# Two network blocks in one kernel: unscaled activations in `w_up` and `w1_1`, and 32 units of the modulation added up by VectorE

## The reference, cut to what matters

```python
def rmsnorm(x, g):                       # r = rsqrt(mean(x*x) + EPS), one number a token
    return x * r * g
def conv_ffn(xn, w_up, conv_w, conv_b, w_down):       # xn = rmsnorm(h, norm_ffn_g)
    h = xn @ w_up                                     # 256 x 5632
    h = causal_conv3(h, conv_w) + conv_b              # per channel, over the tokens
    a, b = jnp.split(h, 2, axis=-1)
    return (jax.nn.silu(a) * b) @ w_down
# second block, two layers i = 0, 1
sx1, cx1, gx1, sx2, cx2, gx2 = split(silu(c) @ ada_w[i] + ada_b[i], 6)       # for x
sc1, cc1, gc1, sc2, cc2, gc2 = split(silu(c_ctx) @ ada_w[i] + ada_b[i], 6)   # for the context
x = x + gx2 * _mlp(_rms(x, norm_mlp_g[i]) * (1 + cx2) + sx2, mlp_w1[i], mlp_w2[i])
def _mlp(h, w1, w2):
    return jnp.square(jax.nn.relu(h @ w1)) @ w2
```

## Time and profile before

| | |
|---|---|
| median of 3 runs | 1424.33 us (1420.19 to 1426.97) |
| the profiled execution's own time | 1423.98 us |
| its span, first to last instruction | 1422.2 us |
| PE busy | 1366.4 us, 96% |
| DVE, ACT, POOL busy | 714.1, 604.7, 448.6 us |
| mean granted clock of TensorE | 0.989 of 2.4 GHz |
| `w_up` on PE | about 243 to 396 us of the span |
| `ab_in`, `ab_out`, `w1_0a` | 474 to 568, 590 to 635, 644 to 733 us |
| `w1_1` | from about 1228 us |

### The profile page before, as it was taken

One profiled execution on the slowest core, in us unless ns is written; L12 is line 12 of the kernel. 1 busy time (PEld: TensorE's weight loads), 2 busy tenths in 40 slices (PEclk: granted clock), 3 DMA queues, 4 the chain that ended last, 5 costly groups with the idle time before them and its releaser, 6 DMA issues.

```text
span 1422.2 us, 20872 instructions
## 1 busy us (share of the span) xinstructions
PE 1366.4 (96%) x8436; PEld 1158.2 (81%) x8436; DVE 714.1 (50%) x1129; ACT 604.7 (43%) x997; POOL 448.6 (32%) x440
## 2 busy tenths in 40 slices
PE   7889999999999999998999999999899999899999
PEld 7777788789999677875788888888577777799999
DVE  7575447757765635227122232222657766844443
ACT  6334445556664322225332133322445544665432
POOL 4532121333342000314440024401266643477200
PEclk9999999999999999999999999999999999999999
DMA  7346567686555445245533332323522221455552
GB/s 279 118 167 206 194 228 242 216 299 234 178 178 179 180 166 173 87 137 184 172 100 93 100 100 93 103 90 104 207 97 96 79 101 45 163 166 187 182 182 85
DMA packets 63968, 220.14 MB, mean 155 GB/s; under 512 B 6912, under 2 KB 10240, under 8 KB 63872
## 3 DMA queue, kind: packets, MB, share of 16 engines
q1 hardware_dynamic: 63584, 218.56, 46.2%
q10 hardware_dynamic: 288, 0.25, 0.1%
HBM read 217.73 MB, written 1.05 MB: 154 GB/s over the span
## 4 chain that ended last, share of the span: by engine, by line
PE 80%; DVE 9%; POOL 4%; ACT 3%; issue 2%; DMA 1%; SPq 0%; DVEq 0%; POOLq 0%; ACTq 0%
PE ps L476 23%; PE ps L490 22%; PE ps L488 22%; PE ps L532 3%; DVE wlo L1419 2%; PE ps L795 1%; POOL tmp L2144 1%; PE ps L822 1%; PE ps L742 1%; PE ps L809 1%; DVE tmp L1685 1%; DVE tmp L1687 1%; DVE Alo L1832 1%; PE ps L483 1%; PE ps L788 1%
## 5 line engine op out<-in xcount | busy, mean ns | idle before, releaser
L476 PE MATMUL ps<-Ahi,whi 128*128 128x256 f32 (+1 forms) x1656 | 552.6, 334 | 16.6 <-ACT Ahi L942 7.0
L490 PE MATMUL ps<-Ahi,wlo 128*128 128x256 f32 (+1 forms) x1584 | 509.2, 321 | 2.2 <-DVE wlo L1419 2.2
L488 PE MATMUL ps<-Alo,whi 128*128 128x256 f32 (+1 forms) x1584 | 509.4, 322 | 0.7 <-DVE Alo L1433 0.5
L1419 DVE TENSOR_TENSOR wlo<-raw,whi 128x1024 fp32r<-128x1024 f32 x298 | 373.3, 1261 | 226.6 <-ACT whi L913 226.5
L913 ACT ACTIVATE whi<-raw 128x1024 fp32r<-128x1024 f32 x305 | 320.2, 1052 | 263.9 <-PE ps L490 217.5
L476 PEld LDWEIGHTS ps<-Ahi,whi 128*128 128x128 f32 x1656 | 319.4, 193 | 93.8 <-issue 40.8
L490 PEld LDWEIGHTS ps<-Ahi,wlo 128*128 128x128 f32 x1584 | 305.2, 193 | 24.8 <-DVE wlo L1419 3.3
L488 PEld LDWEIGHTS ps<-Alo,whi 128*128 128x128 f32 x1584 | 305.4, 193 | 23.6 <-issue 1.9
L488 PE MATMUL ps<-Hlo,whi 128*128 128x256 f32 (+2 forms) x752 | 240.0, 319 | 0.4 <-DVE Hlo L1433 0.4
L476 PE MATMUL ps<-Hhi,whi 128*128 128x256 f32 (+2 forms) x712 | 229.0, 322 | 0.0
L490 PE MATMUL ps<-Hhi,wlo 128*128 128x256 f32 (+2 forms) x712 | 228.6, 321 | 0.0
(11 more groups left out here) (257 smaller groups left out, 1244.9 us busy)
## 6 DMA issues: line engine op xcount, KB each, us to landing
raw<-in_ada SPq DMA_DIRECT2D x96, 512.0 KB, 3.6
raw<-in_w SPq DMA_DIRECT2D x64, 512.0 KB, 3.5
raw<-in_w_up SPq DMA_DIRECT2D x44, 512.0 KB, 4.4
raw<-in_w_in SPq DMA_DIRECT2D x38, 512.0 KB, 4.5
raw<-in_w_0a SPq DMA_DIRECT2D x32, 512.0 KB, 3.5
raw<-in_w_0b SPq DMA_DIRECT2D x32, 512.0 KB, 3.5
raw<-in_na_in SPq DMA_DIRECT2D x24, 512.0 KB, 6.0
raw<-in_w_down SPq DMA_DIRECT2D x22, 512.0 KB, 3.5
```

Source lines behind the costliest of these rows:

```text
L476: e.matmul(o, w_hi, ah, start=k == 0, stop=False)
L488: e.matmul(o, w_hi, al, start=False, stop=False)
L490: m = e.matmul(o, w_lo, ah, start=False, stop=last)
L1419: e.tensor_tensor(wlo[i % NRAW][:, :cols], raw[i % NRAW][:, :cols], plain(whi[s % NHI][:, :cols]), SUB).then_inc(S("wlo").sem, 1)
```

## The change

1. `EARLY` goes from 4 to 44 chunks for `w_up` and from 3 to 32 for `w1_1`: all chunks multiply with the unscaled activations. The normed activations of both stages are gone, and every chunk gets `rescaled` on VectorE (in `w1_1` also the copy of the shift's column, and 258 columns on TensorE). The conv's taps now read `Y` in SBUF in all chunks, where chunks 4 to 43 read PSUM. The five `low` that GpSimd did for these stages go to VectorE.
2. The ada units move. `w_up` has 12 in place of 18, `ab_in` and `ab_out` none inside in place of 20, `w1_0a` 8 ahead of it in place of 6 and 2 behind `ab_out`'s last unit. Units 56 to 87 (`MOD`) stand singly behind every second unit of `w1_0a`, `w2_0a`, `w1_0b`, `w2_0b`. VectorE adds them up, weighted by the condition (`mod_unit`), and TensorE sums the four totals over the partitions with `pick`: 8 matmuls in `w1_0a`, 4 in `w1_0b`, 4 in `na_in`.
3. In both programs the loop that issued `hi` and `lo` for the ada units between `ab_out` and `w1_0a` is gone.

```diff
-ADA_BEFORE = {"ab_in": 6, "w1_0a": 6, "na_in": 8}
-ADA_AFTER = {"w_in": (16, 48), "w_out": (0, 48), "w_up": (2, 48), "ab_in": (0, 88), "ab_out": (4, 88),
-             "w1_0a": (0, 88)}
+ADA_BEFORE = {"ab_in": 6, "w1_0a": 8, "na_in": 8}
+ADA_AFTER = {"w_in": (16, 48), "w_out": (0, 48), "w_up": (2, 42)}
+MOD = range(56, 88)
+MOD_AFTER = ("w1_0a", "w2_0a", "w1_0b", "w2_0b")
+MOD_SUMMED = {("w1_0a", 15): 3, ("w1_0b", 15): 4, ("na_in", 1): 5}
-EARLY = {"w_in": 3, "w_up": 4, "w1_1": 3}
+EARLY = {"w_in": 3, "w_up": 44, "w1_1": 32}
...
+        def mod_unit(n, i):          # VectorE
+            quad, k, pair = n // 16, n // 2 % 8, n % 2
+            first = n in (56, 57) or k == 0
+            vectors = 2 if quad == 3 else 1
...
+            for v in range(vectors):
+                total = modsum[pair][v]
+                if first:
+                    d = e.tensor_scalar(total, raw[i % NRAW], cond[:, k, v:v + 1], None, MUL, ALU.bypass)
+                else:
+                    w.wait_ge(S("mod"), n - MOD.start - 1)
+                    d = e.scalar_tensor_tensor(total, raw[i % NRAW], cond[:, k, v:v + 1], total, MUL, ADD)
+            d.then_inc(S("mod").sem, 1)
...                                  # ScalarE and VectorE, ahead of norm_whole / shifted_hi of m0
-        for i in range(UNIT["ab_out", 7] + 1, before("w1_0a")[0]):
-            his(i)
-        for i in range(UNIT["ab_out", 7] + 1, before("w1_0a")[0]):
-            ada_place(i)
...                                  # VectorE, w_up
-                if n < 4:
-                    rescaled("n1", "w_up", n, rst[:, LEFT])
-                    norm1_steps(*((0, 3), (3, 6), (6, 10), (0, 0))[n])
-                    w.wait_ge(S("resc_w_up"), n + 1)
-                    o = Y[n][:, :256]
-                else:
-                    o = product("w_up", n)[:, :256]
+                if n >= 4:
+                    w.wait_ge(S("up_conv"), n - 3)
+                rescaled("n1", "w_up", n, rst[:, LEFT])
+                w.wait_ge(S("resc_w_up"), n + 1)
+                o = Y[n % 4][:, :256]
```

More of the change, by code:

```diff
@@ L79, in weight_plan @@
                 n += 2
+            if name in MOD_AFTER and u % 2 == 0:
+                assert n in MOD
+                plan.append(("ada", n))
+                n += 1
     assert n == ADA_STEPS
@@ L101, in walk @@
             i = UNIT[name, blk // 8] + 1
-            while name in ADA_AFTER and PLAN[i][0] == "ada" and i not in before(next_stage(name)):
+            while (name in ADA_AFTER or name in MOD_AFTER) and PLAN[i][0] == "ada" and i not in before(next_stage(name)):
                 yield "ada", i
@@ L280, in launch_program @@
     tmp = [sb(f"tmp{i}", 512) for i in range(6)]
-    rst = sb("rst", 512)
+    ssum = sb("ssum", 512)
+    modsum = [[sb(f"modsum{pair}{v}", 1024, at=here[0] + 4096 * (2 * v + pair)) for v in range(2)] for pair in range(2)]
     X = [sb(f"X{i}", 512) for i in range(2)]
     Y = [sb(f"Y{i}", 512) for i in range(4)]
-    ssum = sb("ssum", 512)
+    rst = sb("rst", 512)
     ssum_g = sb("ssum_g", 256)
@@ L404, in load @@
             cols = dram[name].shape[2]
-            if i >= NRAW:
+            if i >= NRAW and PLAN[i - NRAW][0] == "ada" and PLAN[i - NRAW][1] in MOD:
+                w.wait_ge(S("mod"), PLAN[i - NRAW][1] - MOD.start + 1)
+            elif i >= NRAW:
                 w.wait_ge(S("mm"), UNIT_DONE[i - NRAW])
@@ L476, in linear @@
                     e.matmul(o, w_hi, ah, start=k == 0, stop=False)
-                    if kt == 8 and n == early:
+                    if kt == 8 and n == early and name not in ("w_up", "w1_1"):
                         low_ready(s)
@@ L532, in ada_unit, with mod_summed @@
                 m = e.matmul(ps[7][q:q + 32, :], cond[:, k, :], raw[slot][:, 512 * j:512 * j + 512],
-                             start=k == 0, stop=k == 7)
+                             start=k == 0 or i in (88, 89), stop=k == 7 and i < 48)
             m.then_inc(S("mm").sem, 1)
+        def mod_summed(name, n):
+            if (name, n) not in MOD_SUMMED:
+                return
+            quad = MOD_SUMMED[name, n]
+            vectors = 2 if quad == 3 else 1
+            w.wait_ge(S("mod"), min(16 * quad + 16, MOD.stop) - MOD.start)
+            w.wait_ge(S("pick"), 2)
+            if quad == 4:
+                w.wait_ge(S("ada_copy"), 4)
+            for v in range(vectors):
+                for pair in range(2):
+                    for j in range(2):
+                        q = 32 * (2 * pair + j)
+                        m = e.matmul(ps[7][q:q + 32, :], pick[:, v, :], modsum[pair][v][:, 512 * j:512 * j + 512],
+                                     start=quad == 4, stop=v == vectors - 1)
+            m.then_inc(S("mod_sum").sem, 1)
         def ada_following(name, u):
@@ L1080, in scalar_program @@
                     after_out(7)
-        n1_x = [tmp[4], X[0], X[1]]
         def silu(m):
@@ L1213, in scalar_program @@
                 his(UNIT["ab_out", i])
-            if what == "ada" and i < UNIT["ab_out", 7]:
-                his(i)
             if what == "chunk":
@@ L2069, in gpsimd_program @@
         e.memset(cond, 0.0).then_inc(S("cond0").sem, 1)
+        e.memset(pick, 0.0).then_inc(own.sem, own.up())
+        w.wait_ge(own, own.n)
+        for v in range(2):
+            e.memset(pick[:, v, v:v + 1], 1.0).then_inc(S("pick").sem, 1)
         low("w_in", 2)
@@ L2230, in gpsimd_program @@
         parts("m1", ssum[:, :256], lambda c: sq[c % 2][:, :256])
-        for u in (2, 3, 4):
-            low("w1_1", u)
         hidden("h1", 32, 256, "r1")
```

152 lines of the change are left out of this document (55 added, 97 removed), and 6 rows, old and new, of the table IN_TURN.

## The result

| | before | changed |
|---|---|---|
| median | 1424.33 us | 1430.82 us (1428.58 to 1434.65, 9 runs) |
| ratio | 1 | 1.0050, 95% interval 1.0033 to 1.0068 |
| profiled execution's span, mean clock | 1422.2 us, 0.989 | 1428.1 us, 0.983 |

1429.5 us were forecast. The kernel is half a per cent slower, just inside what was called no change. One of four executions of experiment 4 took 5239.6 us; it is left out here, which makes the median there 1409.6 us, where expectations recorded later have 1410.1 and a gain of 20.8.

The account below looks back on a forecast made before the run. PE, busy 96% of the span, was taken to bound the kernel, with `w_up`'s ring out of slack against it. The terms +14.2 - 15.0 + 4.5 + 7.8 - 6.0 = +5.5 us gave 1429.5 us, range 1413 to 1440.

Parts of the forecast that it names:

- its ring: In `w_up`, VectorE, ScalarE and GpSimd making the hidden activations in turn, with no slack left against PE.
- a term of 14.2: `w_up` ends 14.2 us later because the rescale lengthens VectorE's steps; bounds +7.5 to +22.4.
- odd step: VectorE's step for an odd chunk of `w_up`: 3.21 us with rescaling, 2.05 before.
- even step: VectorE's step for an even chunk of `w_up`: 3.91 us with rescaling, 3.74 before; bounds 3.74 and 4.3.
- the sum of squares: GpSimd's sum for the context, needed in `w_down`: PE's wait for it stays 13.1 us behind VectorE's end.
- Rival A: In `w_up` the rescale hides and PE keeps the pace: 1405 us; chance 0.10.
- Rival C: PE's clock falls in `w_up`'s waits, costing 62 us more: 1490 us; chance 0.04.
- Rival D: Light case: even steps unchanged, GpSimd's sum in time, full clock in `w1_0a`: 1420 us; chance 0.13.
- Rival B: In `w_up` the VectorE and GpSimd lock costs its full price, even steps 4.3 us: 1438 us; chance 0.25.
- Part 2: Ada units: 13 pairs leaving PE's path give -15.0 us, sums over the partitions cost +4.5, VectorE's additions stay hidden.
- Part 3: Start of `w1_0a`: PE waits for the later `hi` and `lo`, then runs slow: +7.8 us, bounds +5.1 and +9.7.
- Part 4: `w1_1`: the 4.50 us wait and slow matmuls go, 258 columns cost +0.6: -6.0 us, bounds -7.5 and -4.

Follow-up runs that it names:

- experiment 4: Changed kernel with VectorE's rescale ahead of `lo` in `w_up` from chunk 1 on: 1409.6 us, ratio 0.9887.
- experiment 1: Changed kernel with `w_up` as before the change (4 early chunks): 1412.4 us, ratio 0.9903.
- experiment 5: `resc_even`: changed kernel with VectorE's rescale ahead of `lo` in the even chunks of `w_up` alone: 1419.8 us, ratio 0.9964.
- experiment 7: `low_twice`: changed kernel with GpSimd taking each low part of `w_up` twice: 1437.5 us, ratio 1.0091.
- experiment 9: `ada_back`: changed kernel with 12 groups of four unused matmuls of the ada form behind 12 units of `ab_in`: 1446.5 us, ratio 1.0149.
- up_old_start: Changed kernel with `w_up` as before and `hi` and `lo` of `w1_0a`'s first unit ahead of the norm: 1400.6 us, ratio 0.9832.
- Experiment 3: Changed kernel with `hi` and `lo` of `w1_0a`'s first unit issued ahead of the norm: 1422.3 us, ratio 0.9990.
- experiment 2: Changed kernel with `w1_1` as before the change (3 early chunks): 1440.7 us, ratio 1.0101.
- low_twice_before: Kernel before the change with GpSimd taking each low part of `w_up` twice: 1426.1 us, ratio 1.0015.

## Why the prediction was right

**The bound.** The stage that decides the sign was `w_up`, by its ring, as the prediction had it: 13.8 us by the traces for a term of 14.2, odd step 3.21 for 3.21, even step 3.86 for 3.91, pair 7.07 for 7.12, the sum of squares 13.1 us behind VectorE's end for 13.1. Rival A is out: experiment 1 gets 18.4 us back. Rival C too: the clock was 1.00 over the stage. Rival D would have needed even steps of 3.74 us, GpSimd's sum in time and the full clock in `w1_0a`, and none of the three came.

**Rival B, full exclusion at 4.3 us a step.** It did not come, though the exclusion is real. Its price was wrong: the waiting instruction doesn't need its whole usual duration behind the other's end. A tap ends 0.28 us behind it (usual 0.48), `lo` 1.08 us (usual 1.22), and GpSimd's instructions of 256 columns 0.59 us (usual 0.74). The Trainium skill (SBUF — State Buffer, "SBUF: two separate sides") says that the one which starts first gets the ports for its whole instruction; experiment 5 agrees in either direction (`lo` 1.72 us, low part 1.08), and experiment 7 too (tap 0.84). The 4.3 us were my reading of it, that the loser pays its whole duration again; with the 0.28 us of these rows the exclusion gives 3.87 us, and 3.86 were measured. I also read it only in one direction. The larger price was GpSimd's multiply waiting for VectorE's `lo` (1.58 for 0.74 us), in both kernels; it stood in the earlier trace rows as 1.60, and I took it for the length of the work.

**Part 2.** Nine pairs of ada units left `ab_in` and `ab_out`, and 11.0 us went: 1.22 each for 1.15, and 1.21 by experiment 9. VectorE's additions take 55.0 us in 32, 1.7 each, and the eight that open a total 1.0 each (1.2 was the estimate and 2.4 the upper bound); PE has no wait between 667 and 1000 us. From chunk 1 of `w1_0a` to the end of `na_in` the traces lie 1.5 us further apart (-3.3 + 2.6 + 2.2), where four pairs and three sums were to give -4.6 + 4.5; 0.9 of it is a wait of PE in `na_in`, whose transposes of the modulation now stand behind VectorE's copy of a head. The rest of that is not explained.

**Part 3.** +8.2 us for +7.8, by two errors that cancel. `hi` began at 656.55, which is 1.9 us later than forecast (649.9, and 4.8 of shift). 1.4 of it is the row sum, which was said not to move. It began 0.8 us late (645.34 for 639.72, less 4.8) and took 1.7 us for 1.1, and the ada units just ahead of it took 2.9 us for 1.9, since the clock had fallen (0.50 from 643.5 to 645.3 us). What PE did before differs in one thing: ahead of the squares it now waits 0.84 us, where a pair of ada units had stood. That the wait made the clock fall is not shown. All eleven profiles with this order have the wait; nine show slow ada units behind it, and `low_twice` and `up_old_start` do not. The delay was made up behind the `lo`: from 660.48 to chunk 1 there were 6.9 us and not 8.0. I had charged fourteen slow steps from the `lo` on, but the slow time, 5.9 us as in the earlier trace rows, ran from the first matmul at 657.69, and 2.8 of it passed in the wait for `lo`. Experiment 3 returns 6.5 us by the traces, 8.5 by the medians, by moving one `hi` and one `lo`.

**Part 4** is the term that was mis-sized: -8.6 us by the traces of before and after, and 8.3 by experiment 2's, outside the bounds of -7.5 to -4. There were three errors of one sign. Eight matmuls of old chunk 3 had run ahead of the wait, from 1235.83 on, so that the 4.05 us behind it were 16 matmuls and not 24: 4.50 + (4.05 - 1.92) + 0.93 = 7.6. The first chunk's wait for the low part of the shifted input also went, which makes 0.7 us with the slower matmul behind it. And 258 columns cost nothing over 256, where I had charged 0.6:

```profile
1246.38 0.28 PE L490 MATMUL ps<-Ahi,whi 128*128 128x258 f32 x1
...
1249.26 0.28 PE L490 MATMUL ps<-Ahi,whi 128*128 128x258 f32 x1
```

A chunk takes 2.88 us, as with 256 (1250.02 to 1252.90 in the kernel before). 7.6 + 0.7 are 8.3 of the 8.6 us.

That the total was 1.3 us from the forecast is luck in part. Part 4 gave 2.6 us more than forecast and the nine pairs 0.7 more. The 2.0 us that the profiled execution lost ahead of `w_up` and the 1.6 more of part 2 made up for that.

## What to carry to other kernels

In a ring of several engines that work in order, ask of each instruction whether it has time to lose; put the one that has (here `lo`) behind the one that another engine waits for (here the rescale), and the same instructions cost 21.2 us less. Where an instruction takes twice what the same shape takes elsewhere, as GpSimd's multiply did, it may be waiting inside its recorded time: look at what the other of VectorE and GpSimd issued just before. And when a change removes the loop that issued early what the next stage needs first, put that back ahead of the long norm: 6.5 to 8.5 us hung on the place of two instructions here.

## What the runs showed of the hardware

- Float32 instructions of VectorE with two SBUF inputs and of GpSimd with SBUF inputs exclude each other in either direction, by turns (`resc_even`, `low_twice`). On VectorE the loser ends 0.28 us (254 or 255 columns) or 1.08 us (1024 columns) behind the winner, on GpSimd 0.59 us (256 columns). With one input in PSUM VectorE's taps keep their 0.48 us (`low_twice_before`). The wait is recorded as duration and not as idle time.
- Four matmuls of 32 x 512 in float32 cost PE 1.21 us in the midst of others, 0.99 of it in their own stretch (`ada_back`).
- A chunk of 24 matmuls takes 2.88 us with 258 columns as with 256.
- In `w_up` PE waits of 0.73 us, one a pair, left the granted clock at 1.00 (PE 89% busy). Behind 8.71 us without work it was 0.50 for 5.9 us, with 0.43 in place of 0.23 us a matmul. Behind a wait of 0.84 us ahead of `w1_0a` it fell in nine profiles of eleven.
